# Two norms computed with one root, and first pairs multiplied high parts first, in a two-block fp32 transformer kernel

## The chip, the cores and the metric

The kernel runs on one core of a Trainium2 chip. Its time is the device time of one execution in microseconds (us): 2674.2 us is the median of 3 runs (2673.95 to 2677.19). All times below that are read from a profile come from one execution recorded by the hardware profiler.

## What is computed

Two transformer blocks on 256 tokens of width 2048, in fp32, one after the other. What matters here is the seam between them, and the norm ahead of the second block's feed-forward part:

```python
# end of the first block
    x = x + u @ w_ff2
    x = rmsnorm(x, g_final)                     # norm "n3b"
# start of the second block
    mod = silu(c) @ w_ada + b_ada               # shift_m, scale_m, gate_m, shift_f, scale_f, gate_f
    h = rms_norm(x, g_mix2) * (1 + scale_m) + shift_m      # norm "n3"
    proj = h @ w_in_2                           # stage "in2"
    ...
    x = x + gate_m * (concat([attn, ssm]) @ w_out)         # stage "out2"
    h = rms_norm(x, g_ffn) * (1 + scale_f) + shift_f       # norm "n4"
    x = x + gate_f * conv_ffn(h, w_up, ..., w_down)        # stages "up" and "down" of "ffn"
    return rms_norm(x, g_out)                   # norm "n5"
# rmsnorm(x, g) = x * rsqrt(mean(x*x) + 1e-6) * g
```

With r = 1/sqrt(mean(x²) + eps) and the first norm's gain g, the second norm's mean is r² · mean((x g)²), and the product of both factors is 1/sqrt(mean((x g)²) + eps · mean(x²) + eps²).

## The kernel before

**Tiles.** Activations lie transposed: 2048 channels are 16 chunks of 128 partitions x 256 tokens. X holds x. A matrix product is computed in units: one unit is 128 output channels, 16 chunks deep. Two units (par 0 and 1) make a pair, with its own PSUM bank each.

**High and low parts.** Precision beyond TensorE's fast fp32 format is had by splitting: each operand is rounded to a high part, and the rest is the low part. H and U hold, per chunk, 256 columns high and 256 columns low. In `unit` (lines 278 to 299) each chunk costs two matmuls: w_hi times all 512 columns, and w_lo times the 256 high columns into the bank's second half. The two halves of the bank are added afterwards.

**Weights.** SyncE streams raw weights into four slots of 1024 columns (two per unit). ScalarE casts a slot to w_hi (`cast_high`), VectorE subtracts to w_lo (`split_low`), and TensorE waits for `w_split`. There is one set of four slots in w_hi and w_lo, so a slot is cast anew only after TensorE has signalled `piece_used` for it. In `plain` and the other per-unit functions ScalarE first takes the bank's second half (`take_half`, line 558), then casts the next pair's two slots of the same par; VectorE first adds the halves (line 908, 1253 or 1409), then subtracts.

**Norms.** Squares are summed over chunks into `ss` by VectorE; a matmul with a matrix of ones sums over partitions (`sum_squares`), ScalarE takes the root (`root`, line 565), VectorE the reciprocal (`inverse`, line 940). At the seam, `ssg` holds the sum of (x g_final)². The first root and reciprocal come from ss; ssg's sum is then multiplied by the square of that, and a second root (line 767) and reciprocal follow. `modulated` (lines 1225 to 1237) then makes h: VectorE writes x·g·R into one of four work tiles (line 1230), ScalarE rounds it plus shift into H's high part (lines 770 and 855), and VectorE subtracts for the low part (line 1236), chunk k and the low part of chunk k-1 in turn. TensorE waits for the low part of every second chunk (`h_ready`).

**Around them.** ff2_unit and gated_unit are the units of the stages just before the norms; in their last pair they still cast and subtract the slots of the next stage's first pair. `add_ada` and `take_mod` compute mod beside the other work (line 922, 932, 935). There is no scheduler: each engine runs its instructions in the order in which its block of the program lists them, and semaphores order the engines.

## Time and profile before

| what | us |
|---|---|
| median of 3 runs | 2674.2 |
| span of the profiled execution | 2671.0 |
| TensorE busy | 2589.1 (97%) |
| VectorE busy | 2059.6 (77%) |
| ScalarE busy | 1326.5 (50%) |

The span runs from the first to the last recorded instruction. The profiled execution's own time is its span and what lies around it; between the span and the median of the runs there are 3.2 us. A matmul's recorded duration overlaps the next one's, so the distance between two starts is what one costs, and the engine's busy share is not its share of peak. In timeline rows the number in square brackets is the idle time just before the instruction, and behind the arrow is what ended it. "PEclk" in a row of windows is TensorE's granted clock as a share of 2.4 GHz.

### The profile page before, as it was taken

To read this page: it belongs to the slowest core of one execution; us is meant where nothing else is said; L and a number is where in the kernel's file an instruction comes from. 1 tells how busy PE (TensorE), PEld (TensorE's weight loads), DVE (VectorE), ACT (ScalarE), POOL (GpSimd) and SP (SyncE) were. 2 spreads that over 40 slices of the span, in tenths; PEclk is the share of its full clock that TensorE was granted. 3 is DMA by queue.
4 is the path that set the end of the run, shared out by engine and by line. 5 is a ranking of instruction groups with operands and counts; after the bars stand their busy time and mean duration, and the time that the engine had idled before them with its cause. 6 is when DMAs were issued, how large, how long until landed. Compare 5 with 4: busy or idle time off the path is not lost.

```text
span 2671.0 us, 48348 instructions
## 1 busy us (share of the span) xinstructions
PE 2589.1 (97%) x14656; PEld 2248.0 (84%) x14656; DVE 2059.6 (77%) x2984; ACT 1326.5 (50%) x2048; POOL 5.2 (0%) x13
## 2 busy tenths in 40 slices
PE   7999999999999999999998999989899999999997
PEld 6888888888888888888886888868688888888886
DVE  7678675588887887887888556776788888888888
ACT  5344444565553444443554436644545545545456
POOL 0000000000000000000000000000000000000000
PEclk9999999999999999999998999999899999999999
DMA  7686673557788878778886544414455655656654
GB/s 281 225 281 206 223 263 126 169 189 253 253 282 272 269 267 275 273 270 276 269 271 203 172 152 156 162 64 154 137 186 166 203 190 167 198 183 183 197 169 160
DMA packets 160250, 560.85 MB, mean 210 GB/s; under 512 B 17955, under 2 KB 18252, under 8 KB 160204
## 3 DMA queue, kind: packets, MB, share of 16 engines
q1 hardware_dynamic: 132140, 458.52, 51.7%
q10 hardware_dynamic: 27648, 100.68, 11.6%
q0 software_dynamic: 416, 1.06, 0.2%
q8 instruction: 26, 0.43, 0.1%
q14 instruction: 20, 0.16, 0.0%
HBM read 558.08 MB, written 2.11 MB: 210 GB/s over the span
## 4 chain that ended last, share of the span: by engine, by line
PE 93%; DVE 4%; ACT 1%; issue 1%; DMA 1%; DVEq 0%; ACTq 0%; SPq 0%
PE bank L275 92%; DVE w_lo L902 1%; DVE scratch L1230 1%; DVE R L940 0%; ACT w_hi L543 0%; DMA X<-in_x 0%; DMA ada_w<-in_w_ada 0%; DVE ss L971 0%; PE bank L388 0%; ACT H L572 0%; PE bank L379 0%; DVE ss L1334 0%; DVE G L1371 0%; DVE Z L1482 0%; DVE scratch L940 0%
## 5 line engine op out<-in xcount | busy, mean ns | idle before, releaser
L275 PE MATMUL bank<-H,w_hi 128*128 128x512 f32 x4672 | 1663.0, 400 | 31.5 <-DVE H L1236 16.4
L275 PE MATMUL bank<-H,w_lo 128*128 128x256 f32 x4672 | 1318.0, 282 | 0.0
L902 DVE TENSOR_TENSOR w_lo<-w_raw,w_hi 128x1024 fp32r<-128x1024 f32 x900 | 1092.3, 1222 | 142.4 <-ACT w_hi L543 134.5
L275 PEld LDWEIGHTS bank<-H,w_hi 128*128 128x128 f32 x4672 | 885.2, 189 | 245.5 <-issue 26.3
L543 ACT ACTIVATE w_hi<-w_raw 128x1024 fp32r<-128x1024 f32 x900 | 910.3, 1050 | 1.1 <-DMA w_raw<-in_w_up 0.6
L275 PEld LDWEIGHTS bank<-H,w_lo 128*128 128x128 f32 x4672 | 891.6, 191 | 0.1
L275 PE MATMUL bank<-U,w_hi 128*128 128x512 f32 x1984 | 702.6, 398 | 5.5 <-DVE U L1463 4.8
L275 PE MATMUL bank<-U,w_lo 128*128 128x256 f32 x1984 | 558.8, 282 | 0.0
L558 ACT ACTIVATE scratch<-bank 128x256 f32<-128x256 f32 x356 | 136.9, 385 | 846.2 <-PE bank L275 846.1
L275 PEld LDWEIGHTS bank<-U,w_hi 128*128 128x128 f32 x1984 | 373.1, 188 | 98.4 <-DVE U L1463 6.1
L275 PEld LDWEIGHTS bank<-U,w_lo 128*128 128x128 f32 x1984 | 374.7, 189 | 0.0
L908 DVE TENSOR_TENSOR scratch<-bank,scratch 128x256 f32<-128x256 f32 x324 | 137.5, 424 | 197.7 <-ACT scratch L558 195.3
L922 DVE SCALAR_TENSOR_TENSOR Z<-ada_w,silu_c,Z 128x1024 f32<-128x1024 f32 x192 | 245.4, 1278 | 5.7 <-issue 3.2
L558 ACT ACTIVATE scratch<-bank,mod 128x256 f32<-128x256 f32 x80 | 38.0, 475 | 129.8 <-PE bank L275 129.8
L275 PE MATMUL bank<-B,w_hi 128*128 128x512 f32 x256 | 88.9, 392 | 0.0
L1409 DVE SCALAR_TENSOR_TENSOR scratch<-bank,mod,scratch 128x256 f32<-128x256 f32 x80 | 38.7, 484 | 52.1 <-ACT scratch L558 51.3
L275 PE MATMUL bank<-B,w_lo 128*128 128x256 f32 x256 | 71.7, 280 | 0.0
L1253 DVE TENSOR_TENSOR Z<-bank,scratch 128x256 f32 (+1 forms) x32 | 13.6, 425 | 75.1 <-ACT scratch L558 75.1
L869 ACT ACTIVATE U<-scratch 128x256 f32 x44 | 18.4, 418 | 86.4 <-DVE scratch L1460 86.4
L865 ACT ACTIVATE scratch<-scratch 128x256 f32<-128x256 f32 x44 | 18.4, 419 | 84.1 <-DVE scratch L1441 84.1
L275 PEld LDWEIGHTS bank<-B,w_hi 128*128 128x128 f32 x256 | 48.1, 188 | 10.7
L1438 DVE SCALAR_TENSOR_TENSOR scratch<-scratch,vec 128x255 f32<-128x255 f32 x88 | 42.6, 484 | 12.8 <-DVE scratch L1436 0.2
(199 smaller groups left out, 1230.4 us busy)
## 6 DMA issues: line engine op xcount, KB each, us to landing
w_raw<-in_w_ff SPq DMA_DIRECT2D x256, 512.0 KB, 4.9
ada_w<-in_w_ada ACTq DMA_DIRECT2D x192, 512.0 KB, 4.4
w_raw<-in_w_up SPq DMA_DIRECT2D x176, 512.0 KB, 4.1
w_raw<-in_w_z SPq DMA_DIRECT2D x96, 512.0 KB, 4.6
w_raw<-in_w_in SPq DMA_DIRECT2D x88, 512.0 KB, 4.0
w_raw<-in_w_gate SPq DMA_DIRECT2D x64, 512.0 KB, 4.6
w_raw<-in_w_down SPq DMA_DIRECT2D x64, 384.0 KB, 3.1
w_raw<-in_w_down SPq DMA_DIRECT2D x64, 320.0 KB, 3.3
```

The lines of the kernel that those rows point to most:

```text
L275: return nc.tensor.matmul(out, lhsT, rhs, start=start, stop=stop, skip_group_check=True)
L543: A(w_hi[:, slot, :], w_raw[:, slot, :], ACT.Copy).then_inc(sem("w_high"), 1)
L558: A(half[par], bank[par][:, T:2 * T], ACT.Copy, scale=scale).then_inc(sem("halves"), 1)
L865: A(sig[0], conv[0], ACT.Sigmoid).then_inc(sem("up.sig"), 1)
L869: A(ob(U, i, 0), wide[0], ACT.Copy).then_inc(sem("u_high"), 1)
L902: TT(w_lo[:, slot, :], w_raw[:, slot, :], w_hi[:, slot, :].bitcast(F32), ALU.subtract)\
L908: TT(out, bank[par][:, 0:T], half[par], ALU.add).then_inc(sem("bank_read"), 1)
L922: STT(ada_acc[:, :], ada_w[:, par, :], silu_c[:, bass.ds(k, 1)], ada_acc[:, :], ALU.mult, ALU.add)\
L1230: STT(work(4 + k % 4), xb(k), gain[:, k:k + 1], R[:, :], ALU.mult, ALU.mult)\
L1253: TT(zb(block), bank[par][:, 0:T], half[par], ALU.add).then_inc(sem("bank_read"), 1)
L1409: STT(total[par], bank[par][:, 0:T], mod[:, bass.ds(gate + block, 1)], half[par], ALU.mult, ALU.add)\
L1438: STT(conv[par][:, 1:T], u[:, 0:T - 1], V("ffn_w", 88 + m), conv[par][:, 1:T], ALU.mult, ALU.add)\
```

## The change

1. At the seam both norms share one root. VectorE joins the sums, ssg = eps·ss + ssg, one matmul sums over partitions, and one root with bias eps² and one reciprocal give the product of both factors. The first norm's own factor (still wanted for x) is computed later: its root after the high parts of h, its reciprocal after the first six pairs of in2.
2. In the last unit before n3 and n4, slot 2 of the next pair is cast and subtracted before the unit's own half is taken and added, and slot 3 after the squares. TensorE's sums for n3b, n4 and n5 wait for VectorE's last addition itself, not for a further signal.
3. `modulated` writes x·g·R of all 16 chunks into free blocks of Z without waits, then makes all 16 low parts.
4. The first pair of in2 and of the FFN is multiplied by a new function `pair_high_first`: for each chunk, as soon as its high part is there, w_hi and w_lo times the high columns for both units (four matmuls of 256 columns); then for each chunk w_hi times the low columns for both units. `piece_used` is signalled only in the second loop.
5. The copy of relrow and g2 move behind n3; ScalarE loads the table for the root before the last down units.

```diff
+            def pair_high_first(pair, operand_base):
+                for par in range(2):
+                    pe.wait_ge(sem("bank_read"), 2 * pair + par + 1)
+                for k in range(NC):
+                    h, lhs = k // FIRST_CHUNKS, slice(k % FIRST_CHUNKS * P, (k % FIRST_CHUNKS + 1) * P)
+                    if k % FIRST_CHUNKS == 0:
+                        pe.wait_ge(sem("w_split"), CREDIT + 4 * pair + h + 3)
+                    pe.wait_ge(sem("h_high"), operand_base + k + 1)
+                    for par in range(2):
+                        mm(bank[par][:, 0:T], w_hi[:, 2 * par + h, lhs], H[:, k, 0:T], k == 0, False)
+                        mm(bank[par][:, T:2 * T], w_lo[:, 2 * par + h, lhs], H[:, k, 0:T], False, False)
+                for k in range(NC):
+                    h, lhs = k // FIRST_CHUNKS, slice(k % FIRST_CHUNKS * P, (k % FIRST_CHUNKS + 1) * P)
+                    pe.wait_ge(sem("h_ready"), operand_base + k + 1)
+                    for par in range(2):
+                        end = mm(bank[par][:, T:2 * T], w_hi[:, 2 * par + h, lhs], H[:, k, T:2 * T], False, k == NC - 1)
+                        if k == FIRST_CHUNKS - 1 and par == 0:
+                            end.then_inc(sem("piece_used"), 1)
+                        if k == NC - 1:
+                            end.then_inc(sem("piece_used"), par + 1)
...
-            sum_squares("n3b")
-            with pe.Fori(0, 6) as i:
-                pair_of_units(PAIR0["in2"] + i, H, NC, "h_ready", CHUNKS["h3"])
+            sum_squares("n3b", "ff")
+            pair_high_first(PAIR0["in2"], CHUNKS["h3"])
+            with pe.Fori(1, 6) as i:
+                pair_of_units(PAIR0["in2"] + i, H, NC)
...
+            pair_high_first(PAIR0["ffn"], CHUNKS["h5"])
+            ffn_group(0, 1)
+            with pe.Fori(1, FFN_GROUPS) as g:
                 ffn_group(g)
-            ffn_group(FFN_GROUPS - 1)
-            sum_squares("n5")
+            sum_squares("n5", "down")
...
+            def load_sqrt():
+                A(small[:, 16:17], epsb[:, 0:1], ACT.Sqrt)
...
-            def ff2_unit(pair, par, m, block, chunk, squares=False):
+            def ff2_unit(pair, par, m, block, chunk, squares=False, last=False):
+                if last:
+                    cast_high(pair + 1, par, 0)
                 take_half(pair, par)
-                cast_high(pair + 1, par, 0)
-                cast_high(pair + 1, par, 1)
+                if not last:
+                    cast_high(pair + 1, par, 0)
+                    cast_high(pair + 1, par, 1)
                 if squares:
...
+                if last:
+                    cast_high(pair + 1, par, 1)
...
-            root("n3")
-            act.wait_ge(sem("n3.inverted"), 2)
-            A(std, work(0), ACT.Sqrt, bias=epsb[:, :], scale=1.0 / D).then_inc(sem("norm.root"), 1)
+            root("n3", eps=1)
             for k in range(NC):
                 act.wait_ge(sem("normed"), k + 1)
-                A(H[:, k, 0:T], work(4 + k % 4), ACT.Identity, bias=mod[:, k:k + 1]).then_inc(sem("h_high"), 1)
+                A(H[:, k, 0:T], zb(16 + k), ACT.Identity, bias=mod[:, k:k + 1]).then_inc(sem("h_high"), 1)
+            root("n3b", src=bank[7])
...
+                def second(i, par, last=False):
...
+                    if last:
+                        split_low(pair + 8 + i + 1, par, 0)
+                    n = add_halves(pair + 8 + i, par, total[par])
...
+                if final:
+                    for par in range(2):
+                        second(7, par, par == 1)
+                    dve.wait_ge(sem("ff.ss"), 1 + NC)
+                    dve.wait_ge(sem("ff.ssg"), 1 + NC)
+                    STT(ssg, ss[:, :], EPS, ssg, ALU.mult, ALU.add).then_inc(sem("norm.squares"), 1)
                 take_mod(2 * g + 5)
...
+            split_low(PAIR0["in2"], 1, 1)
...
+            def modulated(gain, shift, chunks, normed):
+                for k in range(NC):
+                    STT(zb(16 + k), xb(k), gain[:, k:k + 1], R[:, :], ALU.mult, ALU.mult).then_inc(sem("normed"), 1)
+                for k in range(NC):
+                    dve.wait_ge(sem("h_high"), chunks + k + 1)
+                    dve.wait_ge(sem("normed"), normed + k + 1)
+                    STT(H[:, k, T:2 * T], zb(16 + k), mod[:, shift + k:shift + k + 1], H[:, k, 0:T].bitcast(F32),
+                        ALU.add, ALU.subtract).then_inc(sem("h_ready"), 1)
...
-            inverse("n3", R2)
-            TT(work(1), R2, R2, ALU.mult).then_inc(sem("n3.inverted"), 1)
-            dve.wait_ge(sem("norm.summed"), NTH["n3b"])
-            dve.wait_ge(sem("n3.inverted"), 1)
-            TT(work(0), bank[7][:, 0:T], work(1), ALU.mult).then_inc(sem("n3.inverted"), 1)
-            inverse("n3b")
-            TT(R[:, :], R[:, :], R2, ALU.mult).then_inc(sem("n3.inverted"), 1)
-            dve.wait_ge(sem("n3.inverted"), 3)
-            modulated(g1, 0, CHUNKS["h3"], 0)
+            inverse("n3")
+            modulated(g1, 0, CHUNKS["h3"], 0)
...
             with dve.Fori(0, 6) as i:
                 for par in range(2):
                     plain_unit(PAIR0["in2"] + i, par, 2 * i + par)
+            inverse("n3b", R2, bank[7][:, T:2 * T])
```

gated_unit and gated (the units of out2) take the same `last` argument. How the instructions then stand, at three places:

VectorE, last unit of ff2, before (908 adds the bank's halves, 1200 adds to x, 902 makes w_lo, 1148 and 1207 sum the squares):

```order
L908 TENSOR_TENSOR scratch<-bank,scratch 128x256
L1199 REGISTER_ALU
L1200 ISA
L1200 TENSOR_TENSOR X<-X,scratch 128x256
L901 REGISTER_ALU
L902 TENSOR_TENSOR w_lo<-w_raw,w_hi 128x1024
L901 REGISTER_ALU
L902 TENSOR_TENSOR w_lo<-w_raw,w_hi 128x1024
L1146 REGISTER_ALU
L1148 TENSOR_TENSOR ss<-ss,scratch 128x256
L1207 TENSOR_TENSOR scratch<-scratch 128x256
```

and now (951 adds the halves, 945 makes w_lo, 1264 joins the sums, 983 is the reciprocal):

```order
L945 TENSOR_TENSOR w_lo<-w_raw,w_hi 128x1024
L951 TENSOR_TENSOR scratch<-bank,scratch 128x256
L1245 TENSOR_TENSOR X<-X,scratch 128x256
L1192 TENSOR_TENSOR ss<-ss,scratch 128x256
L1254 TENSOR_TENSOR scratch<-scratch 128x256
L1264 SCALAR_TENSOR_TENSOR scratch<-ss,scratch 128x256
L975 MEMSET Z 128x1024
L978 TENSOR_TENSOR mod<-bank,vec 128x8
L1271 SCALAR_TENSOR_TENSOR g<-mod,vec 128x16
L1272 TENSOR_TENSOR g<-g,vec 128x16
L945 TENSOR_TENSOR w_lo<-w_raw,w_hi 128x1024
L983 RECIPROCAL R<-bank 128x256
```

One w_lo now stands ahead of the addition and the other ahead of the reciprocal; both stood between the addition and the squares.

VectorE from the reciprocal at the seam to h, before:

```order
L940 RECIPROCAL scratch<-bank 128x256
L1241 TENSOR_TENSOR scratch<-scratch 128x256
L1244 TENSOR_TENSOR scratch<-bank,scratch 128x256
L940 RECIPROCAL R<-bank 128x256
L1246 TENSOR_TENSOR R<-R,scratch 128x256
L1230 SCALAR_TENSOR_TENSOR scratch<-X,g,R 128x256 x2
L1236 SCALAR_TENSOR_TENSOR H<-scratch,mod,H 128x256
```

and now:

```order
L983 RECIPROCAL R<-bank 128x256
L1280 SCALAR_TENSOR_TENSOR Z<-X,g,R 128x256 x16
L1284 SCALAR_TENSOR_TENSOR H<-Z,mod,H 128x256 x16
L1290 COPY Z<-bank 8x384
L1291 SCALAR_TENSOR_TENSOR g<-mod,vec 128x16
```

One reciprocal and three products are gone from the row, and the low parts stand behind all 16 first products.

TensorE, from the sums at the seam on, before (512 columns are high and low together):

```order
L275 MATMUL bank<-ss,ones 128x256
L275 MATMUL bank<-scratch,ones 128x256
L445 UNCONDITIONAL_BRANCH
L445 ISA
L287 ISA
L275 MATMUL bank<-H,w_hi 128x512
L275 MATMUL bank<-H,w_lo 128x256
```

and now, where the sum of both norms comes first, and, behind the three dots' place, the end of the pair:

```order
L275 MATMUL bank<-scratch,ones 128x256
L275 MATMUL bank<-ss,ones 128x256
L275 MATMUL bank<-H,w_hi 128x256
L275 MATMUL bank<-H,w_lo 128x256
L275 MATMUL bank<-H,w_hi 128x256
...
L275 MATMUL bank<-H,w_lo 128x256
L275 MATMUL bank<-H,w_hi 128x256 x32
L471 UNCONDITIONAL_BRANCH
```

All matmuls of the pair are 256 columns wide, and the 32 with the low columns stand last.

## Rows read from the trace of the kernel before

**Rows 1.** The page: busy time of the engines, and the chain by engine.
```profile
PE 2589.1 (97%) x14656; PEld 2248.0 (84%) x14656; DVE 2059.6 (77%) x2984; ACT 1326.5 (50%) x2048; POOL 5.2 (0%) x13
PE 93%; DVE 4%; ACT 1%; issue 1%; DMA 1%; DVEq 0%; ACTq 0%; SPq 0%
```
**Rows 2.** Timeline around n3: start, duration, engine, line, operation, count, idle before.
```profile
1445.19 0.38 ACT L558 ACTIVATE scratch<-bank 128x256 f32<-128x256 f32 x1 [2.67 <-PE bank L275]
1446.55 2.36 DVE L902 TENSOR_TENSOR w_lo<-w_raw,w_hi 128x1024 fp32r<-128x1024 f32 x2
1450.78 1.22 PE L275 MATMUL bank<-ss,ones 128*128 128x256 f32 x2 [2.91 <-DVEq L1152]
1452.62 1.76 DVE L940 RECIPROCAL scratch<-bank 128x256 f32<-128x256 f32 x1 [0.66 <-ACT bank L565]
1458.16 0.88 DVE L1230 SCALAR_TENSOR_TENSOR scratch<-X,g,R 128x256 f32<-128x256 f32 x2
1460.65 0.77 PE L275 MATMUL bank<-H,w_hi 128*128 128x512 f32 x1 [7.80 <-DVE H L1236]
```
**Rows 3.** Timeline, TensorE: first matmul of in2's second unit, and of its second pair.
```profile
1472.33 0.39 PE L275 MATMUL bank<-H,w_hi 128*128 128x512 f32 x1
1477.88 0.39 PE L275 MATMUL bank<-H,w_hi 128*128 128x512 f32 x1
```
**Rows 4.** Timeline around n4: x, sum, the FFN's first matmul, its second pair's.
```profile
1897.45 0.42 DVE L1414 TENSOR_TENSOR X<-X,scratch 128x256 f32 x1
1900.59 1.22 PE L275 MATMUL bank<-ss,ones 128*128 128x256 f32 x2 [4.53 <-DVEq L1152]
1906.68 0.77 PE L275 MATMUL bank<-H,w_hi 128*128 128x512 f32 x1 [4.87 <-DVE H L1236]
1924.02 0.40 PE L275 MATMUL bank<-H,w_hi 128*128 128x512 f32 x1
```
**Rows 5.** Windows: length, PE, PEld, DVE, ACT, POOL busy (count), PEclk, DMA, GB/s.
```profile
1465.00:1467.00 2.00, 1.58 (x7) 0.90 (x5) 2.00 (x6) 1.42 (x3) 0.00 (x0) 0.76 0.00 0
1912.00:1914.00 2.00, 1.97 (x8) 1.13 (x6) 2.00 (x7) 1.25 (x3) 0.00 (x0) 0.72 0.00 0
```
**Rows 6.** Timeline in the FFN's first pair: ScalarE's half, VectorE's slots 0 and 2.
```profile
1918.57 0.39 ACT L558 ACTIVATE scratch<-bank 128x256 f32<-128x256 f32 x1
1919.94 1.23 DVE L902 TENSOR_TENSOR w_lo<-w_raw,w_hi 128x1024 fp32r<-128x1024 f32 x1 [0.53 <-ACT w_hi L543]
1927.32 1.22 DVE L902 TENSOR_TENSOR w_lo<-w_raw,w_hi 128x1024 fp32r<-128x1024 f32 x1
```
**Rows 7.** Timeline and windows: thin matmuls, a pause, and the clock after each.
```profile
981.66 1.95 PE L275 MATMUL bank<-ones,Z 128*128 128x1 f32 x16
1809.64 0.50 PE L275 MATMUL bank<-H,w_hi 128*128 128x512 f32 x1 [3.30 <-DVE H L1349]
981.00:989.00 8.00, 7.99 (x43) 6.84 (x42) 6.39 (x9) 3.01 (x5) 0.00 (x0) 0.79 0.88 299
1806.00:1815.00 9.00, 5.70 (x23) 4.65 (x23) 6.87 (x14) 4.28 (x8) 0.00 (x0) 0.81 0.01 2
```
**Rows 8.** Timeline at n5: the table load, and the sum's matmul.
```profile
2659.21 1.28 ACT L565 ACT_TABLE_LOAD   x1
2659.36 0.70 PE L275 MATMUL bank<-ss,ones 128*128 128x256 f32 x2 [2.51 <-DVEq L1152]
```
**Rows 9.** Timeline, in2's last six pairs: two halves a unit apart; VectorE before.
```profile
1556.74 0.39 ACT L558 ACTIVATE scratch<-bank 128x256 f32<-128x256 f32 x1 [3.38 <-PE bank L275]
1562.39 0.39 ACT L558 ACTIVATE scratch<-bank 128x256 f32<-128x256 f32 x1 [3.37 <-PE bank L275]
1551.61 0.42 DVE L1253 TENSOR_TENSOR Z<-bank,scratch 128x256 f32 x1 [4.41 <-ACT scratch L558]
```
**Rows 10.** Weight loads: shortest, median, longest (ns); window over wn's matmuls (no POOL column).
```profile
L275 PEld LDWEIGHTS bank<-H,w_hi x4672: 186/187/337, 10.8 to 2593.7; 128*128 128x128 f32 x195
116.00:116.50 0.50, 0.50 (x6) 0.50 (x7) 0.00 (x0) 0.00 (x0) 1.00 0.81 328
```

More of the change, by code:

```diff
@@ L123, in build @@
         ones = sb("ones", [P, P])
-        epsb = sb("epsb", [P, 1])
+        epsb = sb("epsb", [P, 2])
         R = sb("R", [P, T])
@@ L835, in _, with gated_unit @@
                 norm_high(k)
-            def gated_unit(name, pair, par, m, block, gate, squares, ahead=True):
+            def gated_unit(name, pair, par, m, block, gate, squares, ahead=True, last=False):
+                if last:
+                    cast_high(pair + 1, par, 0)
                 take_half(pair, par, scale=mod[:, bass.ds(gate + block, 1)])
-                if ahead:
+                if ahead and not last:
                     cast_high(pair + 1, par, 0)
@@ L1250, in plain_unit @@
+            link(STT(g2[:, :], mod[:, 64:80], 1.0, V("g_ffn", 0, 16), ALU.add, ALU.mult))
             def plain_unit(pair, par, block):
@@ L1405, in _, with gated @@
                 low_chunk(k)
-            def gated(name, pair, par, m, block, gate, squares, ahead=True):
+            def gated(name, pair, par, m, block, gate, squares, ahead=True, last=False):
+                if last:
+                    split_low(pair + 1, par, 0)
                 dve.wait_ge(sem("halves"), units_with_half(pair, par))
@@ L1414, in gated @@
                 TT(xb(block), xb(block), total[par], ALU.add).then_inc(sem(name + ".x"), 1)
-                if ahead and squares:
+                if ahead and squares and not last:
                     split_low(pair + 1, par, 0)
-                if ahead:
+                if ahead and not last:
                     split_low(pair + 1, par, 1)
@@ L1420, in gated @@
                     add_square(name, par, block)
+                if last:
+                    split_low(pair + 1, par, 1)
             dve.wait_ge(sem("n3.x"), NC)
             clear_ss("out2")
-            with dve.Fori(0, 8) as i:
+            with dve.Fori(0, 7) as i:
                 for par in range(2):
                     gated("out2", PAIR0["out2"] + i, par, 2 * i + par, 2 * i + par, 32, True)
+            for par in range(2):
+                gated("out2", PAIR0["out2"] + 7, par, 14 + par, 14 + par, 32, True, last=par == 1)
             signal_squares("n4", "out2")
```

102 lines of the change are left out of this document (50 added, 52 removed).

## The prediction

> **What bounds the kernel now.** I read the page's engine table and chain first: TensorE is busy 97% of the span, and the chain that ends last is 93% TensorE [rows 1]. So only two things pay: fewer or faster matmuls, or shorter stretches in which TensorE has nothing to do. The change keeps the multiplied columns, so it can only win in the stretches. The timeline around the two norms that feed a whole stage (n3 ahead of in2, n4 ahead of the FFN) shows them, and so does the end (n5).
>
> At n3 the last matmul of ff2 ends at 1445.15, when ScalarE takes its half [rows 2]. Then follow one behind the other: the last unit's adds, two low-part subtractions (2.36 us), the squares' sums, a matmul for the sum, root, reciprocal, a second sum, root and reciprocal, and the first chunk of h; the first matmul of in2 starts at 1460.65. Its first unit is fed by VectorE, which makes a product and a low part per chunk in turn (scalar_tensor_tensor, STT below), and takes 11.7 us for 16 chunks; its second unit starts at 1472.33, the next pair at 1477.88 [rows 3]. At n4 the same chain has one root: sum 1900.59, first matmul 1906.68, first matmul of the next pair 1924.02 [rows 4].
>
> **The end of the unit before.** In the last unit VectorE subtracts slot 2 before it adds the halves and slot 3 after the squares. At n3 slot 2's subtraction cannot start before add_ada ends (1445.1), so adding starts at about 1446.3 in place of 1445.6 (0.42 us after ScalarE's half plus a wait); then x, two squares on ScalarE (no casts ahead of them), two sums, and the new STT that joins them end at 1449.2. The joined sum's matmul takes 1.22 us [rows 2] to 1450.45, its root 0.45 to 1450.95. VectorE meanwhile clears ada_acc (0.9), adds mod, makes g1 and subtracts slot 3 (1.2): it is free at 1451.95, so here the moved subtraction, not the root, sets the start; the price of that edit is 1.0 us, already in the sum. Reciprocal 1.76 [rows 2], one STT 0.48, one ScalarE op 0.51, with 0.1 of hand-overs: first matmul at 1454.85 in place of 1460.65. Gone are the second reciprocal (as long as the first), three products and one root.
> At n4 VectorE is idle before the half arrives, so slot 2 costs nothing. x is ready at 1897.87 [rows 4]; a square (0.4), its sum (0.42) and hand-overs bring the sum's matmul to 1898.8 in place of 1900.59. Slot 3 is cast behind the square (1.0) and subtracted (1.22) by 1900.65, about 0.5 after the root; then 2.85 as at n3. First matmul at 1903.5 in place of 1906.68.
>
> **The first pair.** It now has 96 matmuls of 256 columns, not 64 of 512 and 256. At full clock 16 (512+256)-column pairs take 5.55 us ([rows 3]: 1472.33 to 1477.88), 0.347 per 768 columns, so 0.116 per 256. At the lower clock, 1.2 GHz, 256 columns are 0.213. TensorE comes out of a pause at the lower clock; it rose 5.3 and 6.2 us after the first matmul (in the middle of the windows with 0.76 and 0.72 [rows 5]). I take 5.5: in it 25.8 matmuls, the other 38.2 of the 64 high ones 4.5, so 10.0; 32 low ones 3.7. The pair takes 13.7 us. VectorE and ScalarE deliver a high chunk per 0.40 us ([rows 2]: two in 0.88), TensorE needs 0.85 or 0.47 for the four matmuls of a chunk, so TensorE sets the pace. The low chunks come behind the 16 high ones: 32 STTs from 1453.75 at 0.40 end at 1466.5, and TensorE wants the last of them at 1468.3, so they are covered by 1.8 us. The pairs end at 1468.55 (n3) and 1917.2 (n4).
>
> **What is late next.** Both units of the pair end together, and all four weight slots are in use until then. ScalarE takes the half, then casts slot 0, then VectorE subtracts it: 1.37 us from ScalarE's half to the subtraction's start, 1.23 for it ([rows 6]: 1918.57, 1919.94), so the next pair's first matmul starts 2.65 after the half, which itself starts 0.2 after the last matmul's start. In before this lay under unit 1; now it is a pause of 2.7 us. Next pair: n3 1471.3 in place of 1477.9, a gain of 6.6; n4 1919.9 in place of 1924.0, 4.1. In the FFN a second wait follows: from the half to the subtraction of slot 2 it takes 8.75 us ([rows 6]: 1918.57 to 1927.32) with a wait for unit 1's half in it, 8.2 without, plus 1.22; TensorE wants slot 2 at 2.65 + 5.65 = 8.3. It waits 1.2. Gain of n4: 2.9. In in2 there is no convolution between, and slot 2 is in time.
>
> **The clock in these pauses.** A pause of 3.30 us (before 1809.64) was followed by the lower clock, 9 us at a mean of 0.81, thus 3.4 us at half and 1.7 us lost; of nine stretches of 1.9 us with only one-column matmuls two were followed by it, as the one at 981.66, 8 us at 0.79 [rows 7]. 2.7 us lies between. Bounds: no loss, or 1.7 at each (at n4 it covers the second wait in part, so about 0.5 more than above). I take half: 1.2.
>
> **The end.** The table load (1.28 from 2659.21) ends 0.43 after the sum's matmul would let the root start (2659.36 + 0.70) [rows 8]. Loaded before the last down units, where ScalarE waits for TensorE, it costs nothing: gain 0.4. The Trainium skill, page "ScalarE: Activation LUTs", section "What ACT_TABLE_LOAD costs", adds 1.38 us of drain to each load; by that the gain here would be 1.8. The trace has the root 0.01 us behind the load, so I keep 0.4.
> The moved reciprocal of n3b (1.76) now stands after six pairs, under about 13 us of small matmuls and unit 6; VectorE idled 4.41 us before the next half [rows 9], so nothing. The same for g2, the row copy and n3b's root.
>
> **The pace of whole stages.** One term does not follow from the code. A unit of 16 chunks takes 5.55 us in some stages and 5.65 in others with the same instructions: in2's first six pairs (1472.33 to 1477.88, [rows 3]) and its last six (ScalarE's halves at 1556.74 and 1562.39, [rows 9]). Over the trace 110 units run at the fast pace and 216 at the slow one; no row tells why. Behind n3, 94 units are fast (first half of in2, out2, FFN groups 1 to 3) and 34 slow (second half of in2, FFN group 0). Bounds: all fast, 3.7 less; all slow, 10.2 more. A fresh draw by the trace's shares costs about 5.4. Nothing says that the stages far from the edit change, so I take a fifth of that: 1.0.
>
> **Sum.** 6.6 + 2.9 + 0.4 = 9.9; less 1.2 (clock) and 1.0 (pace): 7.7. The profiled execution has a span of 2671.0, and the median of the runs is 2674.2; I carry the difference over unchanged. Span 2663.3, time 2666.5.
>
> **Rivals.**
> A. The pause after each first pair is worse than taken: the clock falls in both and VectorE, with both units' results to add at once, is late for slot 1 too. For it: the single set of slots; slot 1 in the FFN is in time by only 0.1 us. Against it: in2 has slack there. Price 1.7 + 0.5 in place of 1.2, plus up to 1.2 for slot 1 and its followers: gain 5.5, 2668.7. 14%.
> B. The stages draw their pace anew: 5.4 in place of 1.0, gain 3.3, 2670.9. For it: the two neighbouring stages of [rows 3, 9] that differ. Against it: FFN groups 1 to 3 all run alike. 17%.
> C. Slower. Each 256-column matmul now has a weight load of its own, and loads set the pace: the load's own duration is 0.19 (0.33 at the lower clock) [rows 10]. Then a first pair's high part takes 14.5 and its low part 6.1, 6.9 more; two pairs 13.8, so 2680.3. It decides above 0.156 us per 256-column matmul at full clock. Against it: 16-column matmuls with their loads pass at 6 to 7 in 0.5 us, so a load and a small matmul need 0.08 [rows 10], and the 256-column matmul of each pair hides a load today. 5%.
> The Trainium skill, page "TensorE: Matmul & The Clock Gate", section "Back-to-back issue gap", says that both operations set the spacing, 81 ns at 128 and 131 ns at 512 columns. At its upper figure the 192 matmuls would cost up to 2.9 us more than by 0.116. The trace has 0.347 for 768 columns, so the 131 is not met here.
> D. It pays more: no fall of the clock and FFN group 0 (22 units, 0.1 each) turning fast: 9.9 + 2.3 = 12.2, 2662.0. 6%.
> The forecast, gains from 5.5 to 10: 58%.
>
> **How the numbers follow.** Both ends leave a tenth out: the low end 2661.5 is D with half a microsecond, the high end 2673.5 is B with a pair of the costs of A. 0.2% is 5.35 us, about what a measurement of this kernel tells from no change: faster means below 2668.9. The forecast, D and half of A are faster, 0.71, less 0.03 for the forecast's lower edge, where a few hand-overs that I left out decide: 0.68. B, the rest of A and that edge are the same, 0.26 after 0.01 of B in which the draw goes all slow. That and C are slower: 0.06.
>
> **What would show it.** Right: one reciprocal between the end of ff2 and in2, begun about 6.8 us after the last matmul (4.6 at n4); first matmuls 9.7 (n3) and 7.4 us (n4) after it; 64 high matmuls without a wait and 32 low ones at 0.116; then a pause of 2.6 us ended by w_lo; in the FFN another of about 1.2 five and a half microseconds on; no table load at the end. Wrong: low matmuls waiting for H (VectorE sets the pace), 256-column matmuls above 0.13, a first pair over 15 us, or units of out2 and FFN groups 1 to 3 at 5.65.

## The result, and the profile after

The changed kernel takes 2661.0 us (median of 4 runs, 2657.0 to 2663.4), the kernel before 2675.4 beside it (4 runs, 2674.0 to 2677.2): ratio 0.9944, interval 0.9931 to 0.9957, so 11.5 to 18.5 us faster. Forecast were 2666.5 and a range from 2661.5 to 2673.5: the direction was right, the size too small, and the median lies 0.5 us below the range.

The profiled execution took 2658.68 us with a span of 2656.9, 14.1 us less than the span of before. What bounds it has not changed:

```profile
PE 2581.8 (97%) x14720; PEld 2252.2 (85%) x14720; DVE 2057.7 (77%) x2983; ACT 1323.2 (50%) x2049; POOL 5.2 (0%) x13
PE 93%; DVE 3%; ACT 2%; issue 1%; DMA 1%; DVEq 0%; ACTq 0%; SPq 0%
```

The timeline around n3, to be held against [rows 2, 3] (start, duration, engine, line, operation, count, idle time before it and its releaser):

```profile
1436.85 0.38 ACT L589 ACTIVATE scratch<-bank 128x256 f32<-128x256 f32 x1 [1.42 <-PE bank L275]
1440.14 0.43 DVE L1264 SCALAR_TENSOR_TENSOR scratch<-ss,scratch 128x256 f32<-128x256 f32 x1
1440.63 0.70 PE L275 MATMUL bank<-scratch,ones 128*128 128x256 f32 x2 [1.09 <-DVE scratch L1264]
1442.30 1.23 DVE L945 TENSOR_TENSOR w_lo<-w_raw,w_hi 128x1024 fp32r<-128x1024 f32 x1
1443.44 1.75 DVE L983 RECIPROCAL R<-bank 128x256 f32<-128x256 f32 x1
1446.40 0.55 PE L275 MATMUL bank<-H,w_hi 128*128 128x256 f32 x1 [4.37 <-ACT H L804]
1456.42 4.00 PE L275 MATMUL bank<-H,w_hi 128*128 128x256 f32 x32
1462.98 0.50 PE L275 MATMUL bank<-H,w_hi 128*128 128x512 f32 x1 [2.56 <-DVE w_lo L945]
```

One sum, one reciprocal, with slot 3's subtraction (1442.30) right ahead of it. From ScalarE's half to the first matmul of in2 it takes 9.55 us in place of 15.46, to the second pair's 26.13 in place of 32.69. The 32 low matmuls (1456.42) run without a wait, then TensorE stands still for 2.56 us until slot 0's low part is there. (ScalarE's half of a unit, "the half" below, is its copy of the bank's second half; the last one of ff2 or out2 is the zero from which the seams are timed.)

At n4 (against [rows 4, 6]), in this trace and then, two rows, in a second trace of the same code:

```profile
1884.62 0.47 ACT L589 ACTIVATE scratch<-bank,mod 128x256 f32<-128x256 f32 x1 [1.71 <-PE bank L275]
1887.04 0.70 PE L275 MATMUL bank<-ss,ones 128*128 128x256 f32 x2 [2.45 <-DVE ss L1192]
1891.60 0.55 PE L275 MATMUL bank<-H,w_hi 128*128 128x256 f32 x1 [3.87 <-ACT H L896]
1907.53 0.50 PE L275 MATMUL bank<-H,w_hi 128*128 128x512 f32 x1 [2.56 <-DVE w_lo L945]
```

```profile
1904.74 0.50 PE L275 MATMUL bank<-H,w_hi 128*128 128x512 f32 x1 [2.56 <-DVE w_lo L945]
1911.63 0.50 PE L275 MATMUL bank<-H,w_hi 128*128 128x512 f32 x1 [0.97 <-DVE w_lo L945]
```

First matmul 6.98 us after the half, the second pair's 22.91, where before had 10.47 and 27.81. Behind it the two traces part. The windows (length, PE, PEld, DVE, ACT, POOL busy with counts, PEclk, DMA, GB/s) show the granted clock at n3, at n4 and behind n4's pause, in the first trace and then in the second:

```profile
1437.00:1463.00 26.00, 17.98 (x119) 16.35 (x119) 22.28 (x49) 11.94 (x27) 1.75 (x3) 0.80 0.20 68
1884.60:1907.50 22.90, 14.07 (x98) 13.49 (x98) 18.66 (x40) 12.55 (x25) 0.00 (x0) 0.85 0.23 73
1907.50:1913.00 5.50, 5.47 (x22) 4.71 (x23) 4.65 (x10) 1.63 (x3) 0.00 (x0) 0.69 0.54 170
```

```profile
1904.70:1913.00 8.30, 7.29 (x39) 6.12 (x40) 7.40 (x13) 4.07 (x7) 0.00 (x0) 1.00 0.43 131
```

In the first the clock falls behind the pause (5.5 us at 0.69, so 1.7 us lost) and the second wait for slot 2 is hidden by it; in the second it stays at full speed and the wait shows, 0.97 us. So the gain to the second pair, 4.90, is not kept: seven units on, where both kernels run 5.65 us a unit, 3.26 are left (3.03 in the second trace). The two pairs also differ in length, 15.93 and 16.46 us, because the clock rose 3.7 us after the first matmul in one and 4.9 in the other.

At the end ([rows 8]) the root now follows the sum at once (2645.65, then 2646.39); the load stands ahead of the final down units:

```profile
2584.16 1.28 ACT L574 ACT_TABLE_LOAD   x1
2645.65 0.70 PE L275 MATMUL bank<-ss,ones 128*128 128x256 f32 x2 [2.45 <-DVE ss L1192]
2646.39 0.45 ACT L596 ACTIVATE bank<-bank,epsb 128x256 f32<-128x256 f32 x1 [0.85 <-PE bank L275]
```

Last half to the end: 13.66 us in place of 14.12, so 0.46.

The three seams together: 6.56 + 3.26 + 0.46 = 10.3 us. The other 3.8 of 14.1 lie in stages whose TensorE instructions are the same in both kernels, and they are a difference of two larger numbers. The changed kernel reaches ff2's last half 8.3 us sooner (1436.85 against 1445.19), before any seam; behind it, the seams set aside, it is 4.5 us slower. One place of the second kind, in2's first half, before and then changed:

```profile
1489.17 0.39 ACT L558 ACTIVATE scratch<-bank 128x256 f32<-128x256 f32 x1 [3.27 <-PE bank L275]
1494.72 0.39 ACT L558 ACTIVATE scratch<-bank 128x256 f32<-128x256 f32 x1 [3.27 <-PE bank L275]
```

```profile
1480.24 0.38 ACT L589 ACTIVATE scratch<-bank 128x256 f32<-128x256 f32 x1 [3.38 <-PE bank L275]
1485.89 0.38 ACT L589 ACTIVATE scratch<-bank 128x256 f32<-128x256 f32 x1 [3.37 <-PE bank L275]
```

A unit takes 5.55 us before and 5.65 now, so of the 6.56 us gained at n3, 5.40 are left at the end of these twelve units. Where the two paces come from was the question for the experiments.

### The profile page after: what moved, and what is told of

It is laid out like the page before. It is cut to its first block, busy times and chain, and to the rows that moved or that the text cites. A ratio compares the mean times of both kernels' runs of the same rounds, so it can differ in the third digit from the quotient of the medians.

```text
span 2656.9 us, 48338 instructions
## 1 busy us (share of the span) xinstructions
PE 2581.8 (97%) x14720; PEld 2252.2 (85%) x14720; DVE 2057.7 (77%) x2983; ACT 1323.2 (50%) x2049; POOL 5.2 (0%) x13
## 4 chain that ended last, share of the span: by engine, by line
PE 93%; DVE 3%; ACT 2%; issue 1%; DMA 1%; DVEq 0%; ACTq 0%; SPq 0%
PE bank L275 92%; DVE w_lo L945 1%; ACT w_hi L570 1%; DVE Z L965 0%; DVE R L983 0%; DMA X<-in_x 0%; DMA ada_w<-in_w_ada 0%; DVE ss L1015 0%; PE bank L413 0%; ACT H L604 0%; PE bank L404 0%; DVE scratch L951 0%; DVE ss L1378 0%; DVE Z L1532 0%; DVE G L1415 0%
## 5 line engine op out<-in xcount | busy, mean ns | idle before, releaser
L275 PE MATMUL bank<-H,w_hi 128*128 128x512 f32 (+1 forms) x4736 | 1654.9, 395 | 28.4 <-DVE w_lo L1002 10.6
```

The costliest lines, as they stand in the source:

```text
L275: return nc.tensor.matmul(out, lhsT, rhs, start=start, stop=stop, skip_group_check=True)
```

## The experiments

Unless told otherwise a run is compared by the mean of its executions; a deviation behind ± is one standard error of that mean. All executions of the kernel before (103, in five comparisons) have the mean 2674.9 ± 0.5 and spread from 2662.8 to 2688.3. The comparisons ran on different chips; the means of the kernel before that were taken beside them lie between 2674.2 and 2677.2, each with an error of 0.8 to 1.4, so runs of different comparisons are set side by side below.

**Both kernels again.** No edit.

> The changed kernel once more, unedited. The seams (stretches between two stages with a norm) must repeat: 26.2 us from ff2's last matmul to the second pair of in2, 22.9 from out2's last matmul to the second pair of the FFN, each within 0.3. What is open is the pace of the long stages, in which the first trace had ff1, v and mix at 5.55 us per pair of 16 chunks and in2's first half and out2 at 5.65. Theory P (the pace belongs to the program, its place in memory or its code): the same stages are fast and slow again, and the span is within 1 us of 2656.9. Theory E (it is drawn anew with each execution or each loading): several stages of 16 units stand otherwise, each worth 1.7 us, and the times of the runs spread by 3 to 7 us.

> The kernel before once more, unedited. Seams as before: 32.7 us (n3) and 27.95 (n4) to the second pair, within 0.3. Theory P: ff1 and v again at 5.65 per unit of 16 chunks, in2's first half and out2 at 5.55, span within 1 us of 2671.0. Theory E: another pattern, span and times 3 to 7 us apart from the first.

Measured: 12 executions each, 2663.0 ± 1.3 (2657.4 to 2669.4) and 2672.0 ± 1.4 (2664.1 to 2680.7). The seams repeated: 26.28 and 23.44 us against 26.13 and 22.91 in the changed kernel (the 0.53 at n4 is more than the 0.3 expected, and comes from the clock's later rise), 32.68 and 27.81 against 32.69 and 27.81 in the kernel before. The paces did not. Two halves of ScalarE, the same in both, one unit apart, in the first and in the second trace of the kernel before:

```profile
323.55 0.39 ACT L558 ACTIVATE scratch<-bank 128x256 f32<-128x256 f32 x1 [3.38 <-PE bank L275]
329.20 0.39 ACT L558 ACTIVATE scratch<-bank 128x256 f32<-128x256 f32 x1 [3.37 <-PE bank L275]
```

```profile
323.56 0.39 ACT L558 ACTIVATE scratch<-bank 128x256 f32<-128x256 f32 x1 [3.27 <-PE bank L275]
329.11 0.39 ACT L558 ACTIVATE scratch<-bank 128x256 f32<-128x256 f32 x1 [3.27 <-PE bank L275]
```

5.65 us in one execution, 5.55 in the other, of one and the same program. Of some 355 gaps between successive halves that have one of the two lengths (3.81 and 3.89 for the 11-chunk units of down), the fast one had 119 in the first trace of before and 219 in the second, 174 and 171 in the two of the changed kernel. Theory P is out for the kernel as a whole, though its number was met once: the changed kernel's second span, 2657.3, is 0.4 from the first, with other stages fast. Theory E holds for many stages; whether they differ by execution or by loading of the program these traces can't tell. It does not hold for all of them. The last ff2 runs at 5.65 in all eleven traces without added small matmuls ahead of n3. In2's first half runs at 5.55 in all four of them whose first pair goes unit after unit, and at 5.65 in five of the six with `pair_high_first` (slot3_later is the sixth; the eleventh trace has small matmuls in this stage, and b_nudged, whose first pair goes unit after unit, also began it at 5.65). The final down units take 3.81 us in both traces of the kernel before and 3.89 in the nine others. So two stages, some 2.3 us together, were slower in every trace of the changed kernel than in both of the kernel before; whether the change does that is not shown.

The difference between the second two traces is 9.3 us, where that of the first two was 14.1. Both, by stretch (kernel before less changed kernel, us):

| stretch | first traces | second traces |
|---|---|---|
| up to ff2's last half | 8.3 | 6.6 |
| the three seams | 10.3 | 9.9 |
| all other stages behind it | -4.5 | -7.2 |
| span | 14.1 | 9.3 |

By the other traces the first row is no work of the change: the nine traces of the changed kernel and its variants without small matmuls ahead of n3 reach that half at 1442.8 us on average (1434.4 to 1448.0), the two of the kernel before at 1443.1.

**The first pairs as before.** `pair_high_first` out, at both places:

```
-            pair_high_first(PAIR0["in2"], CHUNKS["h3"])
+            pair_of_units(PAIR0["in2"], H, NC, "h_ready", CHUNKS["h3"])
-            pair_high_first(PAIR0["ffn"], CHUNKS["h5"])
+            pair_of_units(PAIR0["ffn"], H, NC, "h_ready", CHUNKS["h5"])
```

> The changed kernel with the first pair of in2 and of the FFN's first group multiplied as in the kernel before (unit after unit, each chunk's high and low part together, waiting for the low part of every chunk). Theory 1 (the high-first pair pays about half of each seam): at n3 the first matmul waits for the second chunk's low part and the second unit ends no pause at w_lo; second pair about 3.1 us later than in the changed kernel (29.3 us after ff2's last matmul), at n4 about 3.8 later (26.7), less up to 1.7 if no fall of the clock follows there: in all 5 to 7 us longer than the changed kernel. Rival (the gain comes from the joined root and the squares alone): within 1.5 us of the changed kernel. If the pace of other stages moves with this edit of some instructions of TensorE, theory P or E above adds up to 5 us of either sign, visible stage by stage.

Measured: 2668.7 ± 1.5, so 6.3 ± 1.8 above the 16 executions of the changed kernel (2662.4 ± 1.0). Second pairs 29.10 (n3) and 26.09 us (n4) after the half: 3.0 and 3.2 later than in the changed kernel (at n4 about 1.4 are left two units on, since here no second wait or fall of the clock follows). The reason stands in one row, the first matmul of in2, 15.7 us after the half at 1445.96:

```profile
1461.69 0.77 PE L275 MATMUL bank<-H,w_hi 128*128 128x512 f32 x1 [9.88 <-DVE H L1284]
```

It waits for low parts that now stand behind all 16 products. Theory 1 holds; here making all products first costs time unless TensorE also takes the high parts first.

**Only the joined root.** The changed kernel without the new order in the last units, the products ahead, the high-first pair and the early table load; TensorE's direct wait for the last addition stays:

```
-                        ff2_unit(pair + 15, par, 16 * g + 14 + par, 14 + par, None, True, par == 1)
+                        ff2_unit(pair + 15, par, 16 * g + 14 + par, 14 + par, None, True)
                         (the same for VectorE and out2: no last=)
-            split_low(PAIR0["in2"], 1, 1)
-                if final:
-                    load_sqrt()
                         (pair_high_first -> pair_of_units; one product, one low part in turn)
```

> Of the change only the first part: the two norms behind ff2 joined into one root, with n3b's own root behind in2's first half. Squares stand behind the casts again, h is made chunk by chunk, the first pairs are multiplied as in the kernel before, the table is loaded at the end. Theory 1 (the parts add up seam by seam): at n3 one sum, root, reciprocal and three products less, one STT more: the first matmul of in2 11.8 us after ff2's last half in place of 15.5, the second pair 29.0 in place of 32.7, so 3.7 us; nothing at n4 (27.8) and at the end. Mean time 3.7 below the kernel before. Rival (ScalarE's casts and VectorE's low parts fill the time that the second root leaves, so joining pays nothing without the other parts): second pair 31 us or later, under 2 us gained.

Measured: 2668.8 ± 1.3, 6.1 ± 1.4 below the kernel before. First matmul of in2 11.12 us after the half, second pair 28.33, a gain of 4.36 where 3.7 was expected; at n4 0.8 (26.99), where nothing was expected. 0.7 of it lies ahead of the first matmul: the sum's matmuls, which no longer wait for a further signal, start 0.2 sooner, and they run at full clock, 0.70 us in place of 1.22:

```profile
1898.77 0.70 PE L275 MATMUL bank<-ss,ones 128*128 128x256 f32 x2 [4.24 <-DVE ss L1190]
```

The rival is out. Joining is the largest single part at n3; the other 2.2 us come with the remaining parts together, and without the high-first pair these cost 0.8 (29.10 against 28.33).

**The table load back at the end.**

```
-                if final:
-                    load_sqrt()
```

> The changed kernel with one edit undone: the square root's table is not loaded ahead of the last down units but by the last root itself. Theory 1 (the load costs nothing there and saves 0.44 us at the end): the end 0.44 us longer, nothing else; the final down units stay at 3.89 us each. Theory 2 (the load, which delays ScalarE's half by 0.6 us, is what changed the final down units from 3.81 us in both traces of the kernel before to 3.89 in all four of the changed one and its variants): they run at 3.81 again, 1.2 us less over 16 units, so 0.7 us less in all. Both are below what the times can tell; the trace decides.

Measured: 2665.0 ± 1.1. The end is 14.12 us after the last half, against 13.66: 0.46 longer. The gain also hangs on the clock: in low_by_unit_2 and slot3_later, with the load ahead, the sum's matmuls ran at the lower clock and the end took 14.18. Final down units 3.89 us, as in joined_only, which has the load at the end too, so theory 2 is out. The load and the root behind it:

```profile
2657.26 1.28 ACT L596 ACT_TABLE_LOAD   x1
2658.55 0.45 ACT L596 ACTIVATE bank<-bank,epsb 128x256 f32<-128x256 f32 x1
```

**One unit's slots free sooner.** The low matmuls of the first pair unit by unit:

```
-                for k in range(NC):
-                    ...
-                    pe.wait_ge(sem("h_ready"), operand_base + k + 1)
-                    for par in range(2):
+                for par in range(2):
+                    for k in range(NC):
+                        ...
+                        if par == 0:
+                            pe.wait_ge(sem("h_ready"), operand_base + k + 1)
                         end = mm(bank[par][:, T:2 * T], w_hi[...], H[:, k, T:2 * T], False, k == NC - 1)
-                        if k == FIRST_CHUNKS - 1 and par == 0:
+                        if k % FIRST_CHUNKS == FIRST_CHUNKS - 1:
                             end.then_inc(sem("piece_used"), 1)
```

> The changed kernel with one edit: the 32 low matmuls of each of the two first pairs run unit by unit (all 16 chunks of the first unit, then all 16 of the second), and the first unit's end is told to ScalarE at once. Theory 1 (the 2.56 us pause behind the pair is the time that one slot takes from the last use to the split weights, with nothing beside it): the first unit's slots come free 1.85 us sooner, so the pause falls from 2.56 to about 0.7 at both places, the second pair starts 1.85 us sooner, and the fall of the clock in the FFN's first units goes with it (1.7 us at most): 3.7 to 5.4 us less in all. Rival (VectorE's low parts are late when the first unit takes them at twice the rate, one per 0.116 us against 0.40 delivered): they run out before the last chunk, the pair ends later by up to 1 us and the gain is under 2 us.

> low_by_unit once more, to stand beside nudged on the same chip and to double its runs. Seams again 24.3 (n3) and 22.0 us (n4) from the last half to the second pair; mean time 1 to 4 us below the changed kernel's 2663.0.

The pause behind the pair in in2 and in the FFN, and the second wait there:

```profile
1463.62 0.50 PE L275 MATMUL bank<-H,w_hi 128*128 128x512 f32 x1 [0.76 <-DVE w_lo L944]
1900.46 0.50 PE L275 MATMUL bank<-H,w_hi 128*128 128x512 f32 x1 [0.76 <-DVE w_lo L944]
1907.34 0.51 PE L275 MATMUL bank<-H,w_hi 128*128 128x512 f32 x1 [0.97 <-DVE w_lo L944]
```

2.56 became 0.76; the second pair starts 24.27 (n3) and 21.98 us (n4) after the half, 1.86 and 0.93 sooner, no fall of the clock behind either; the second wait stays. At n4 the other 0.9 went before the pause: the first matmul came 0.2 later, and the clock rose 5.2 us after it in place of 3.7, and half of these 1.4 us of lower clock are lost. The mechanism is as expected, with a trace of the rival: VectorE's low parts, covered by 1.8 us in the changed kernel (its last one ends at 1457.99, TensorE wants it at 1460.2), have no slack left here. The last one ends 0.5 us ahead of ScalarE's half of the first unit, at n3 as at n4, about as long as TensorE's last matmul and the hand-over take:

```profile
1454.06 6.42 DVE L1283 SCALAR_TENSOR_TENSOR H<-Z,mod,H 128x256 fp32r<-128x256 f32 x16
1460.98 0.38 ACT L588 ACTIVATE scratch<-bank 128x256 f32<-128x256 f32 x1 [5.91 <-PE bank L275]
```

But by the times nothing is gained: 2662.4 ± 1.0 in 21 executions, as the changed kernel, a difference of 0.0 ± 1.4. That shuts out the 3.7 to 5.4 us expected, and is two of its errors from the 3.1 that the seams show (1.86, and 1.23 seven units on at n4). What took these back is not shown. With small matmuls in both (below), low_by_unit is 3.9 ± 2.0 us below the changed kernel.

**Slot 3 still later.** On top of that the last low part of the weights behind the fourth product:

```
-            split_low(PAIR0["in2"], 1, 1)
                 for k in range(NC):
                     STT(zb(16 + k), xb(k), gain[:, k:k + 1], R[:, :], ALU.mult, ALU.mult).then_inc(sem("normed"), 1)
+                    if k == 3:
+                        split_low(pair, 1, 1)
                 (and split_low(pair + 1, par, 1) out of out2's last unit)
```

> low_by_unit with one more edit: VectorE makes the low part of the last weight slot not ahead of the reciprocal but behind the fourth product of h, both at n3 and at n4 (TensorE wants it at the ninth chunk). Theory 1 (at n3 that subtraction, not the root, holds the reciprocal back): first matmul of in2 8.6 us after ff2's last half in place of 9.6, of the FFN 6.6 in place of 7.0; second pairs sooner by as much, so 1.4 us. Rival (the products behind it come late by its 1.22 us, and TensorE, at the low clock or not, waits for chunk 5): the second pairs no sooner than in low_by_unit (24.3 and 22.0).

Measured: 2664.5 ± 0.9 (6 executions). The first matmul of in2 came at 8.59 us, as expected, but the first unit ended no sooner (half 21.80 us after ff2's last, against 21.63), and the second pairs came at 24.76 (n3, where the clock fell at 1469.9, during the first pair) and 23.04 us (n4) against 24.27 and 21.98. At n4 the first matmul stayed at 7.19 (6.6 expected). The rival holds: VectorE sets the end of the first unit. Its last low part ends 21.3 us after ff2's last half, 0.2 later than in low_by_unit (1.0 sooner by the start, 1.2 later by the subtraction), at n4 1.1 later, and the half follows it by the same 0.5 us as there:

```profile
1462.92 6.43 DVE L1284 SCALAR_TENSOR_TENSOR H<-Z,mod,H 128x256 fp32r<-128x256 f32 x16
1469.83 0.38 ACT L588 ACTIVATE scratch<-bank 128x256 f32<-128x256 f32 x1 [5.89 <-PE bank L275]
```

**What a pace hangs on.** Small matmuls into an unread bank, and waits, inside stages:

```
+            def nudge(columns):
+                mm(bank[3][:, 0:columns], H[:, 0, 0:P], H[:, 0, 0:columns], True, True)
             (ahead of in2's third to sixth pair: 16, 40, 64, 16 columns;
              of out2's fourth to eighth: 16, 24, 40, 64, 16)
+                pe.wait_ge(sem("halves"), 2 * (PAIR0["in2"] + i) - 16)     (ahead of in2's last six pairs)
```

> The changed kernel with probes on TensorE for the two paces of a unit (5.55 and 5.65 us). In in2's first half and in out2 a matmul of 16, 24, 40 or 64 columns into an unread bank stands ahead of some pairs; in in2's second half TensorE waits, ahead of each pair, until ScalarE has taken the half of the unit before (about 0.3 us of standstill). Theory R (the pace is settled where TensorE starts again after standing still, and kept until it stands still again): no change of pace at the small matmuls, several changes over the six waits. Theory S (it is a phase that any uneven instruction shifts): the pace changes at the small matmuls too. Theory Q (it belongs to the stage and the chip's state in it): no change at either.

Measured: one execution, 2670.0 us; its trace is what counts.

TensorE's timeline around the first small matmul, and ScalarE's halves a unit apart on both sides of it:

```profile
1483.64 0.40 PE L275 MATMUL bank<-H,w_hi 128*128 128x512 f32 x1
1483.88 0.28 PE L275 MATMUL bank<-H,w_lo 128*128 128x256 f32 x1
1484.00 0.17 PE L275 MATMUL bank<-H 128*128 128x16 f32 x1
...
1485.16 0.39 PE L275 MATMUL bank<-H,w_hi 128*128 128x512 f32 x1
1485.39 0.28 PE L275 MATMUL bank<-H,w_lo 128*128 128x256 f32 x1
```

```profile
1478.54 0.39 ACT L597 ACTIVATE scratch<-bank 128x256 f32<-128x256 f32 x1 [4.21 <-PE bank L275]
1484.20 0.38 ACT L597 ACTIVATE scratch<-bank 128x256 f32<-128x256 f32 x1 [3.38 <-PE bank L275]
1489.86 0.39 ACT L597 ACTIVATE scratch<-bank 128x256 f32<-128x256 f32 x1 [3.39 <-PE bank L275]
1495.41 0.38 ACT L597 ACTIVATE scratch<-bank 128x256 f32<-128x256 f32 x1 [3.27 <-PE bank L275]
```

From a 512-column matmul to the next one 0.24 us ahead of it, 0.23 behind; a unit 5.66, then 5.55 (the one at 1489.86 has the small matmul's 0.1 in it). TensorE never stood still there. In all, a small matmul turned a slow pace fast in 2 of 3 cases and a fast one slow in none of 6; over the waits the pace changed once each way. That this stage turns fast at all is most likely the small matmul's doing: in the five traces of in2's first half that enter it slow and have none, it stays slow to the end. Theory S holds best, for the small matmuls. That the pace is a phase of the stream, kept as long as the stream is even, is argued from this and not shown, and what such a phase would be against stays open.

**Small matmuls in all long stages.** On low_by_unit, and then on both kernels of this study, a matmul of 16 and one of 24 columns ahead of the second and third pair of 23 stages:

```
+            def pairs(base, first, n, buf, chunks, *args):
+                for i in range(first, first + 3):
+                    if i > first:
+                        nudge(buf, (16, 24)[i - first - 1])
+                    pair_of_units(base + i, buf, chunks, *args)
+                with pe.Fori(first + 3, n) as i:
+                    pair_of_units(base + i, buf, chunks, *args)
```

> low_by_unit with a matmul of 16 columns ahead of the second and one of 24 ahead of the third pair of each of 23 long stages, into a bank that nobody reads. In the run with the probes such a matmul took 0.13 us; it moved a stage that ran at 5.65 us per unit to 5.55 in 2 of 3 cases and one that ran at 5.55 to 5.65 in none of 6. Theory 1 (a small odd matmul shifts a phase on which the pace hangs, and the fast pace holds): most stages run at 5.55 (down 3.81) from the third pair on; with about 200 of 326 units slow otherwise, 0.1 us each, two thirds of them mended, less 46 times 0.13 us: about 13 less 6, 7 us below low_by_unit. Rival (the two mended cases were chance; each restart of the stream draws the pace anew, both ways): as many slow stages as elsewhere and 6 us longer than low_by_unit.

> The kernel before with the same small matmuls as nudged (16 and 24 columns ahead of a stage's second and third pair, 23 stages). Theory 1 (the pace of the long stages has nothing to do with the change, and most of the spread of the times is this pace): the stages that multiply H run at 5.55, the time is about 8 us below the kernel before, some 2667, as nudged was 7.9 below low_by_unit. Rival (the change itself altered the pace, and the nudges only help behind it): no more than 3 us below, with H stages at 5.65.

> The changed kernel with the same small matmuls. It stands beside b_nudged so that the two kernels are compared with the pace of most stages held equal. Theory 1 (the change's worth is its three seams): 10 us below b_nudged, from 8.5 to 11.5, some 2657. Rival (part of the measured 12 us is a better pace or fewer falls of the clock elsewhere that the change brings with it): 12 us or more below b_nudged.

| kernel | executions | mean, us | without them |
|---|---|---|---|
| before | 12 | 2669.5 ± 0.7 | 2674.9 ± 0.5 |
| changed | 6 | 2659.3 ± 1.4 | 2662.4 ± 1.0 |
| low_by_unit | 6 | 2655.3 ± 1.5 | 2662.4 ± 1.0 |

The last one, 0.9923 of the kernel before (0.9900 to 0.9945), is the fastest of the study. Low_by_unit_2, its neighbour on the same chip, has 2663.2 ± 1.0, so 7.9 ± 1.8 more; the kernel before, compared on one chip, gained 4.7 ± 1.2 by them. In the trace of nudged the stages that multiply H run fast, those that multiply U (mix, ff2, down) mostly stay slow; ff1 and ff2 of one group:

```profile
762.26 0.39 ACT L588 ACTIVATE scratch<-bank 128x256 f32<-128x256 f32 x1 [2.44 <-PE bank L275]
767.81 0.39 ACT L588 ACTIVATE scratch<-bank 128x256 f32<-128x256 f32 x1 [2.43 <-PE bank L275]
854.44 0.38 ACT L588 ACTIVATE scratch<-bank 128x256 f32<-128x256 f32 x1 [3.38 <-PE bank L275]
860.09 0.38 ACT L588 ACTIVATE scratch<-bank 128x256 f32<-128x256 f32 x1 [3.37 <-PE bank L275]
```

Theory 1 holds for low_by_unit and, with a smaller gain, for the kernel before (5.4 ± 0.9 where 8 was expected); the changed kernel's 3.1 ± 1.7 is not clear of noise. With the pace of most stages held equal (178 and 180 fast gaps in the two traces) the change is worth 2669.5 - 2659.3 = 10.2 ± 1.5 us, on one chip. The two traces agree: their spans differ by 10.0 us, their three seams by 10.1. The rival (12 or more) is not shut out by the interval of the times.

## Why the prediction was wrong, point by point

- **n3, gain 6.6.** Right: 6.56. First matmul 9.55 us after the half (forecast 9.7), second pair 16.6 behind it (16.45). That slot 3's subtraction sets the start and not the root is what the rows show, and slot3_later took the 1.0 us away.
- **n4, 4.1 less a second wait.** The wait is there (0.97, forecast 1.2). The gain to the second pair was 4.90, with the first matmul 7.0 and not 7.4 us behind the half; net 3.26 and 3.03 for 2.9.
- **High matmuls.** 0.213 at the lower clock as taken, 0.120 at full clock (1452.82 to 1453.06 for two) where 0.116 was taken; the clock rose 5.1 (n3) and 3.7 us (n4) after the first one where 5.5 was taken for both, and 3.1 to 5.6 over the five traces with this pair. The low parts were in time, as forecast. Rival C needed 0.156. The Trainium skill, "TensorE: Matmul & The Clock Gate", section "Back-to-back issue gap", gives 131 ns for 512 columns; this trace has 0.23 to 0.24 us.
- **The end, 0.4.** Right: 0.46, and as much lost when the load was put back. The Trainium skill, "ScalarE: Activation LUTs", section "What ACT_TABLE_LOAD costs", would have it 1.8 with the drain, an estimate; the root starts 0.01 us behind the load, so there is none here.
- **The clock behind the pauses, 1.2.** Charged too high. Five traces have the pause of some 2.6 us at both seams, and a fall behind it in 2 of the 10 places, both at n4. There it hides the second wait: the first trace, with it, keeps 3.26 us, the second, without, 3.03.
- **The pace of whole stages, 1.0: the term that failed.** The prediction looked only at the stages behind n3, put those ahead of it at nothing, and took a fifth of a fresh draw because nothing said that stages far from the edit change. Stages far from the edit do change, between two executions of one program. Ahead of n3 the changed kernel was 8.3 us sooner in the first pair of traces (6.6 in the second), behind it 4.5 us slower (7.2). In the prediction's sum the term stood as a cost of 1.0; measured it was a gain of 3.8. That is 4.8 of the 6.4 us between the forecast gain of the span, 7.7, and the measured one, 14.1; the clock term is 1.2 and the seams 0.4.

The sum of the seams, 9.9, was right within half a microsecond (10.3, 9.9, and 10.2 with the pace held equal). That the median fell just outside the range is partly luck: a single execution of one kernel spreads by 4 to 5 us (standard deviation), so a median of four lies 2 or 3 us beside its mean, and the 16 executions of the changed kernel have 2662.4 ± 1.0, inside the range. Against the mean of all 103 of before that is 12.4 ± 1.1, two more than the seams explain and four to five more if the two stages that ran slow in every trace of the changed kernel (2.3 us) are a cost of the change. That gap stays open.

Rival B had the mechanism and, behind n3, about the size: 4.5 and 7.2 us against its 5.4. It left out the stages ahead of n3. The prediction named units of out2 or of FFN groups 1 to 3 at 5.65 as a sign of being wrong, and it came: out2 ran at 5.65 in both traces of the changed kernel, FFN groups 1 and 2 in the second. Rival D is near in size (2662.0) and wrong in cause: FFN group 0 stayed slow in the first trace.

## What to carry to other kernels

Where TensorE is busy 97% of the time, add up the seams from the timeline: here that sum came out within half a microsecond. What differs between executions of one program belongs in the range around it, over the whole kernel and not only behind the edit. Before a difference under half a per cent is explained, look at one unit's length in two traces of the same code: here it differs by 1.8%. And making the products of split operands ahead paid only together with multiplying the high parts first; without that it made the seam longer (29.10 us against 28.33).

## What the runs showed of the hardware

- A steady stream of a 512- and a 256-column matmul with their weight loads has two paces, 0.347 and 0.353 us, in the same program, each mostly kept over a whole stage (119 and 219 fast units in two traces of the kernel before). Over some 326 units 0.1 us each makes up to 33 us, an estimate, so it can carry much of the executions' spread of 25 us; how much it does is not shown.
- One matmul of 16 or 24 columns in the stream, 0.1 us longer with it, can turn the slow pace into the fast one. 46 of them took 7.1 ± 1.8 us off low_by_unit. With H as operand it works in nearly all stages, with U hardly; why is open.
- The clock fell behind some stretches of one-column matmuls and not behind others of the same length. In the changed kernel's first trace 2 of the 8 stretches of 16 between 699 and 1345 us were followed by the lower clock, at 1.7 us lost each.
- A pause of some 2.6 us was followed by a fall in 2 of 10 cases, one of 0.76 to 0.86 us in none of 7 (low_by_unit, low_by_unit_2, nudged, and n4 of slot3_later).
